# Added rows follow the scored rows by 24 places instead of 32 in the gather order of an expert layer

## The chip, the cores and the metric

The kernel runs on one core of one Trainium2 chip. The metric is device time in microseconds of one execution of the whole program. All data are fp32.

## The reference

The program computes a chain of transformer-like blocks on 256 tokens with 2048 channels (attention, a Fourier mixer, a convolution and state-space mixer, attention to a memory) and ends with an expert layer (PEER). Only this last layer is touched by the change:

```python
def peer(h, w_q, sub_keys, u_tab, v_tab):
    ...                                    # for each token and each of 8 heads: two top-16 lists, summed,
    top_s, pos = lax.top_k(cand_s, PEER_TOPK)   # and of the 256 sums the top 16
    idx = jnp.take_along_axis(cand_i, pos, axis=-1)
    g = jax.nn.softmax(top_s, axis=-1)
    ...
    def block(args):                       # 128 tokens, 8 x 16 = 128 experts for each
        xt, it, gt = args
        u = jnp.take(u_tab, it, axis=0)
        act = jax.nn.gelu(jnp.einsum("td,tkd->tk", xt, u))
        v = jnp.take(v_tab, it, axis=0)
        return jnp.einsum("tk,tkd->td", gt * act, v)
```

Then the layer's output is added to the residual stream and normalised with a gain. Each table has 16,384 rows of 2048 floats (8 KB).

## The kernel before, in words

The tokens lie in two tiles of 128, one token on each partition. For tile t and slot k (0 to 127, 16 for each head) one gather fetches, for each of the 128 tokens, its own row of a table: 128 rows of 8 KB, at most 1 MB. A gather of the first table (u) brings what is called here a **scored** row: VectorE multiplies it by the token's vector and sums it to one number per token (line 3779, one fused instruction). A gather of the second table (v) brings an **added** row: it is multiplied by its weight and added to the output. Slots with an exactly zero weight get an index beyond the table, and those tokens' rows are left out of the transfer.

- **Gathers** are issued by GpSimd (lines 3892 for u, 3896 for v), in the order that `gather_order` writes out and that all engines follow. There are 12 buffers. Gather n (after the start) takes the buffer of gather n - 12 and waits until that row is used. A scored row's gather waits besides for its head's indices (`idx`); an added row's gather waits for `rows_needed` of its head, the indices in which the zero weights are marked.
- **The order** begins with `LAG` scored rows. Then one added row and one scored row alternate until the scored rows are out; the last `LAG` added rows stand alone.
- **VectorE** (`v_experts`) walks through the same order. A scored row is multiplied and summed. Behind each head's 16th scored row comes `v_cubic` (four small instructions, lines 3739 to 3745), and `WEIGHTS_BEHIND = 4` places later `v_weights` (lines 3754 to 3763), the last of which writes `rows_needed`. The choice of the experts for the next pair of heads is laid beside the scored rows k = 0, 2, ... 18 of each 32 (`choice_at`), in ten steps. After the last added row of a tile `v_finish` adds the sums (line 3790), takes the norm and scales (line 3796).
- **ScalarE** (`a_experts`) computes the tanh for each head right behind that head's last scored row (line 3828), the exponentials of a choice (line 3690), and for each added row that TensorE takes a diagonal matrix with the weights (line 3837, four buffers). It works in order: diagonals behind a tanh wait for the tanh.
- **TensorE** adds the rows: `diag @ row` in four products of 512 columns, which accumulate in four PSUM banks (line 3579). While both kinds of rows alternate it takes the slots with k % 8 = 1 to 7 and VectorE those with k % 8 = 0 (line 3726). Of the rows of the second tile that stand alone (`added_alone`) TensorE takes k % 8 = 1, 3, 5, 7 and VectorE the even ones.

For the first two heads the experts are chosen head by head before the gathers begin; from the third head on a slot whose softmax weight is exactly zero is skipped in the u table as well.

Of the kernel before, what the change touches and what calls it, by code (L numbers as in the profile page):

```python
# [37 lines left out]
E_HEADS, E_KEYS, E_HALF, TOPK = 8, 128, 64, 16  # L38
# [3402 lines left out]
        return [key for q in (ch // 4, ch // 4 + 1) for key in turn_free(("ffn_x", q), 4, NT)]  # L3441


LAG = 2 * TOPK
PE_ROWS = (1, 2, 3, 4, 5, 6, 7)
PE_ROWS_ALONE = (1, 3, 5, 7)
WEIGHTS_BEHIND = 4
# [3 lines left out]
def gather_order():  # L3451

    scored = [(t, 0, k) for t in range(NT) for k in range(E_SLOTS)]
    added = [(t, 1, k) for t in range(NT) for k in range(E_SLOTS)]
    order = scored[:LAG]
    for n in range(len(added)):
        order.append(added[n])
        order += scored[LAG + n:LAG + n + 1]
    return order
# [10 lines left out]
def added_alone(t, k):  # L3470

    return (t, k) >= (NT - 1, E_SLOTS - LAG)

# [579 lines left out]
```

## Time and profile before

| | us |
|---|---|
| median of 3 runs | 3149.53 |
| lowest, highest | 3142.96, 3149.68 |
| the profiled execution, whole | 3139.42 |
| its span from first to last instruction | 3138.1 |
| first gather of the expert layer | 2093.34 |
| last gather issued | 3107.52 |

TensorE is busy for 90% of the span, VectorE for 72%, GpSimd for 37%, ScalarE for 33%. These are averages over stages with different limits. The expert layer is the last third of the span and is read by itself. Places in the code are given as the lines of the kernel (L3892 is line 3892); "releaser" is the instruction or transfer on which a wait ended.

### The profile page before, as it was taken

Reading aid. Unit: us, or ns where it says so; the run is one execution under the profiler, and the core shown is the slowest. Engines: PE = TensorE matmul, PEld = TensorE weight load, DVE = VectorE, ACT = ScalarE, POOL = GpSimd, SP = SyncE. Lnnn points to the kernel's source line nnn. Section 1 sums busy time; section 2 is a strip of 40 time slices with the busy share of each in tenths; the row PEclk is TensorE's granted clock in tenths of the full one; section 3 lists DMA queues with packets and bytes.
Section 4 is the critical chain, followed back from the end, with each engine's and each line's share of the span. In section 5 each row is a group of like instructions: output and inputs, shape, how many; then the busy total and the mean of one; then the engine's idle time right before and its main releaser. Section 6 shows DMA issues by size and latency. Waiting matters only on the chain.

```text
span 3138.1 us, 35531 instructions
## 1 busy us (share of the span) xinstructions
PE 2815.4 (90%) x12772; PEld 1974.2 (63%) x12772; DVE 2259.0 (72%) x3778; ACT 1047.5 (33%) x2133; POOL 1159.5 (37%) x1973
## 2 busy tenths in 40 slices
PE   6999999899999999999999999992888798888888
PEld 4667888556688888787876778882333333333333
DVE  5558888876667776556785565579978878888766
ACT  5454345234355545344523554421000010100001
POOL 6677877870000000000121000027555565554653
PEclk9999999999999999999999999996999899999999
DMA  9977585644647766555454474469999999999996
GB/s 377 387 282 267 213 278 188 242 168 161 199 130 257 244 219 200 182 189 208 155 176 134 165 239 133 174 232 418 417 418 417 418 414 414 402 418 411 417 416 248
DMA packets 297872, 865.10 MB, mean 276 GB/s; under 512 B 30249, under 2 KB 154537, under 8 KB 228009
## 3 DMA queue, kind: packets, MB, share of 16 engines
q1 hardware_dynamic: 216448, 417.56, 38.3%
q0 software_dynamic: 77024, 434.65, 34.1%
q10 hardware_dynamic: 4224, 10.62, 0.9%
q8 instruction: 101, 1.65, 0.2%
q14 instruction: 75, 0.61, 0.1%
HBM read 965.94 MB, written 17.96 MB: 314 GB/s over the span
## 4 chain that ended last, share of the span: by engine, by line
PE 61%; DVE 20%; DMA 12%; ACT 3%; issue 3%; POOL 1%; SPq 0%; ACTq 0%; POOLq 0%; DVEq 0%
PE lin L569 13%; PE lin L3579 8%; PE lin L571 6%; PE lin L494 6%; PE lin L496 6%; PE lin L495 6%; DVE arena L3779 5%; DMA arena<-in_peer_u,arena 4%; PE lin L395 4%; DMA ring<-in_peer_v,arena 3%; DMA ring<-in_peer_u,arena 2%; DVE scratch L916 2%; DMA arena<-in_peer_v,arena 2%; DVE weight_parts L452 2%; DVE ring L3779 1%
## 5 line engine op out<-in xcount | busy, mean ns | idle before, releaser
L452 DVE TENSOR_TENSOR weight_parts<-ring,weight_parts 128x512 fp32r<-128x512 f32 (+2 forms) x994 | 671.3, 689 | 468.2 <-ACT weight_parts L440 463.4
L440 ACT CAST weight_parts<-ring 128x512 fp32r<-128x512 f32 (+2 forms) x994 | 595.4, 609 | 696.9 <-PE lin L496 349.2
L569 PE MATMUL lin<-parts,weight_parts 128*128 128x512 f32 x1792 | 641.0, 401 | 12.7 <-DVE weight_parts L452 9.8
L3579 PE MATMUL lin<-ring,scratch 128*128 128x512 f32 x1136 | 529.8, 621 | 96.5 <-ACT scratch L3837 52.1
L571 PE MATMUL lin<-parts,weight_parts 128*128 128x256 f32 x1792 | 502.7, 281 | 0.0
L3579 PEld LDWEIGHTS lin<-ring,scratch 128*128 128x128 f32 x1136 | 220.6, 199 | 402.3 <-issue 343.3
L494 PE MATMUL lin<-weight_parts,parts 128*128 128x512 f32 (+2 forms) x1092 | 419.3, 384 | 22.3 <-DVE weight_parts L452 15.8
L3779 DVE CUSTOM_DVE_ANT_0 arena<-ring,aux 128x2048 f32<-128x2048 f32 x146 | 333.8, 2286 | 110.8 <-DMA ring<-in_peer_u,arena 106.9
L495 PE MATMUL lin<-weight_parts,parts 128*128 128x512 f32 (+2 forms) x1092 | 409.6, 375 | 0.0
L496 PE MATMUL lin<-weight_parts,parts 128*128 128x512 f32 (+2 forms) x1092 | 409.4, 375 | 0.0
L569 PEld LDWEIGHTS lin<-parts,weight_parts 128*128 128x128 f32 x1792 | 338.0, 189 | 109.8 <-DVE weight_parts L452 15.5
L3579 PE MATMUL lin<-arena,scratch 128*128 128x512 f32 x560 | 266.9, 627 | 106.4 <-ACT scratch L3837 82.7
L571 PEld LDWEIGHTS lin<-parts,weight_parts 128*128 128x128 f32 x1792 | 339.8, 190 | 0.4
L3892 POOL DMA_INDIRECT ring<-in_peer_u,arena x168 | 206.3, 1228 | 331.8 <-DVE arena L3596 230.8
L3579 PEld LDWEIGHTS lin<-arena,scratch 128*128 128x128 f32 x560 | 109.8, 201 | 258.6 <-issue 163.4
L494 PEld LDWEIGHTS lin<-weight_parts,parts 128*128 128x128 f32 x1092 | 207.4, 190 | 75.5 <-DVE weight_parts L452 25.0
L3837 ACT ACTIVATE scratch<-ident,arena 128x128 f32<-128x128 f32 x212 | 79.6, 398 | 507.7 <-PE lin L3579 475.3
L3896 POOL DMA_INDIRECT ring<-in_peer_v,arena x172 | 178.5, 1038 | 185.9 <-PE lin L3579 111.6
L496 PEld LDWEIGHTS lin<-weight_parts,parts 128*128 128x128 f32 x1092 | 207.4, 190 | 36.8
L495 PEld LDWEIGHTS lin<-weight_parts,parts 128*128 128x128 f32 x1092 | 207.8, 190 | 35.0 <-issue 1.1
L3779 DVE CUSTOM_DVE_ANT_0 arena<-arena,aux 128x2048 f32<-128x2048 f32 x74 | 169.2, 2286 | 50.5 <-DMA arena<-in_peer_u,arena 47.0
L1095 POOL DMA_DIRECT2D arena<-mem_turned x3 | 1.6, 543 | 538.9 <-PE aux L2324 528.7
(357 smaller groups left out, 3775.5 us busy)
## 6 DMA issues: line engine op xcount, KB each, us to landing
ring<-in_ada_row_loads SPq DMA_DIRECT2D x64, 1024.0 KB, 7.9
ring<-in_w_in_fourier SPq DMA_DIRECT2D x64, 1024.0 KB, 8.4
ring<-in_ada_front_loads SPq DMA_DIRECT2D x32, 1024.0 KB, 9.0
ring<-in_w_in_attn SPq DMA_DIRECT2D x32, 1024.0 KB, 6.0
ring<-in_w_out_fourier SPq DMA_DIRECT2D x16, 2048.0 KB, 8.1
ring<-in_w_in SPq DMA_DIRECT2D x24, 1024.0 KB, 7.5
ring<-in_mem_k_loads SPq DMA_DIRECT2D x16, 1024.0 KB, 10.9
ring<-in_w_out_attn SPq DMA_DIRECT2D x8, 2048.0 KB, 8.0
```

The costliest lines, as they stand in the source:

```text
L395: mm = c.nc.tensor.matmul(banks[j // 2][:, (j % 2) * SEQ:(j % 2 + 1) * SEQ], wt[:, k % L.kc, j * P:(j + 1) * P], rhs(k), start=(k == 0 and ...
L440: c.nc.scalar.copy(c.w_parts[:, q, 0, 0:L.per * w], weights_of(c, L, load, w, k)).then_inc(c.a_high.after(("high", L.name, i)), 1)
L452: c.nc.vector.tensor_tensor(c.w_parts[:, q, 1, 0:L.per * w], weights_of(c, L, load, w, k), c.w_parts[:, q, 0, 0:L.per * w].bitcast(F32), A ...
L494: c.nc.tensor.matmul(banks[t][:, 0:w], lhs(0, k, t), hi, start=(k % part == 0), stop=False)
L495: c.nc.tensor.matmul(banks[t][:, 0:w], lhs(0, k, t), lo, start=False, stop=False)
L496: mm = c.nc.tensor.matmul(banks[t][:, 0:w], lhs(1, k, t), hi, start=False, stop=(k % part == part - 1))
L569: c.nc.tensor.matmul(pairs(banks[j][:, :]), c.w_parts[:, q, 0, b], x, start=(k == 0), stop=False, skip_group_check=True)
L571: mm = c.nc.tensor.matmul(banks[j][:, hi_at * SEQ:(hi_at + 1) * SEQ], c.w_parts[:, q, 1, b], x[:, hi_at, :], start=False, stop=(k == L.K - ...
L3579: mm = nc.tensor.matmul(X.sums[t][b][:, :], c.diag[:, X.diag_of(t, k), :], X.buf_of[t, 1, k][:, b * 512:(b + 1) * 512], start=(k == PE_ROW ...
L3779: c.nc.vector.tensor_tensor_reduce(out=product, in0=buf, in1=hn, scale=1.0, scalar=0.0, op0=ALU.mult, op1=ALU.add, accum_out=X.act[:, t, k ...
L3892: c.nc.gpsimd.indirect_dma_start(X.bufs[q], None, X.tables[0], rows, bounds_check=E_KEYS * E_KEYS - 1, oob_is_err=False).then_inc(got[q].a ...
L3896: c.nc.gpsimd.indirect_dma_start(X.bufs[q], None, X.tables[1], rows, bounds_check=E_KEYS * E_KEYS - 1, oob_is_err=False).then_inc(got[q].a ...
```

## The change

`LAG` becomes 24 instead of 32. So the order begins with 24 scored rows, an added row follows the scored row of the same slot by 24 slots and not 32, and the last 24 added rows (k from 104 to 127 of the second tile) stand alone. The functions `gather_order` and `added_alone` read `LAG`; nothing else is edited.

```diff
-LAG = 2 * TOPK
+LAG = TOPK + TOPK // 2
 PE_ROWS = (1, 2, 3, 4, 5, 6, 7)
 PE_ROWS_ALONE = (1, 3, 5, 7)
 WEIGHTS_BEHIND = 4
```

## Rows read from the trace of the kernel before

**Rows 1.** Busy time by stage: us, PE, PEld, DVE, ACT, POOL, PEclk, DMA share, GB/s

```profile
2100.00:2125.00 25.00, 24.32 (x118) 21.04 (x117) 24.36 (x46) 2.13 (x5) 17.85 (x9) 1.00 1.01 422
...
2170.00:2690.00 520.00, 417.51 (x896) 174.35 (x896) 426.42 (x648) 47.77 (x133) 298.93 (x267) 0.91 1.01 417
2690.00:2715.00 25.00, 14.97 (x29) 6.59 (x30) 21.89 (x38) 6.42 (x15) 7.79 (x8) 0.73 0.96 368
2715.00:3065.00 350.00, 298.20 (x643) 124.31 (x642) 268.45 (x371) 30.17 (x84) 194.91 (x184) 0.94 1.01 416
3065.00:3115.00 50.00, 45.92 (x104) 19.98 (x103) 41.39 (x27) 7.72 (x19) 24.27 (x23) 0.97 0.88 325
3115.00:3138.10 23.10, 12.33 (x29) 5.13 (x27) 6.07 (x13) 3.10 (x9) 0.00 (x0) 0.88 0.11 46
```

**Rows 2.** DMA queue of the gathers: packets, MB, share of 16 engines

```profile
q0 software_dynamic: 77024, 434.65, 34.1%
```

**Rows 3.** Waits, 2100 to 3138.1 us: total us, times, longest

```profile
POOL ring L3896 <- PE lin L3579: 111.6, 72, 4.4
DVE arena L3779 <- DMA ring<-in_peer_u,arena: 106.9, 79, 2.9
...
DVE arena L3779 <- DMA arena<-in_peer_u,arena: 47.0, 36, 2.1
```

**Rows 4.** Timeline of the end: start us, us, engine, instruction

```profile
3047.31 0.99 POOL L3892 DMA_INDIRECT arena<-in_peer_u,arena  x1 [0.30 <-issue]
...
3063.18 0.99 POOL L3896 DMA_INDIRECT arena<-in_peer_v,arena  x1 [1.15 <-PE lin L3579]
...
3065.07 2.29 DVE L3779 CUSTOM_DVE_ANT_0 arena<-arena,aux 128x2048 f32<-128x2048 f32 x1 [1.78 <-DMA arena<-in_peer_u,arena]
...
3070.43 15.70 PE L3579 MATMUL lin<-ring,scratch 128*128 128x512 f32 x32 [4.08 <-ACT scratch L3837]
...
3073.79 0.17 DVE L3763 CAST arena<-arena 128x16 uint32<-128x16 f32 x1
...
3127.37 2.48 DVE L3790 TENSOR_TENSOR arena<-arena,lin 128x512 f32<-128x512 f32 x4 [12.58 <-PE lin L3579]
...
3070.43 56.91 PE lin L3579 x128
```

**Rows 5.** Timeline of GpSimd: the gathers 0, 23, 24, 27, 31 and 32

```profile
2093.34 1.07 POOL L3892 DMA_INDIRECT ring<-in_peer_u,arena  x1 [230.75 <-DVE arena L3596]
...
2144.01 0.99 POOL L3892 DMA_INDIRECT arena<-in_peer_u,arena  x1 [0.30 <-issue]
2145.31 2.14 POOL L3892 DMA_INDIRECT ring<-in_peer_u,arena  x1 [0.30 <-issue]
...
2154.05 0.99 POOL L3892 DMA_INDIRECT ring<-in_peer_u,arena  x1 [2.98 <-DVE arena L3779]
...
2166.76 2.28 POOL L3892 DMA_INDIRECT ring<-in_peer_u,arena  x1 [3.57 <-DVE arena L3779]
2169.34 1.91 POOL L3896 DMA_INDIRECT arena<-in_peer_v,arena  x1 [0.30 <-issue]
...
2193.68 3.01 POOL L3892 DMA_INDIRECT ring<-in_peer_u,arena  x1 [0.30 <-issue]
```

**Rows 6.** Timeline of VectorE: end of scored row 15, weights of head 0

```profile
2153.18 0.08 DVE L3779 DVE_READ_ACCUMULATOR2_ANT arena<- 128x1 f32 x1
...
2163.59 0.17 DVE L3763 CAST arena<-arena 128x16 uint32<-128x16 f32 x1
```

**Rows 7.** Busy time from the first gather's traffic on, columns of rows 1

```profile
2094.00:2159.10 65.10, 40.73 (x223) 35.31 (x221) 63.37 (x136) 8.72 (x23) 47.35 (x29) 0.85 0.99 403
```

**Rows 8.** The same in 2 us windows; the gain row's load

```profile
2094.00:2096.00 2.00, 2.00 (x11) 1.74 (x10) 1.86 (x10) 0.00 (x0) 1.42 (x2) 1.00 0.56 61
2096.00:2098.00 2.00, 2.00 (x11) 1.77 (x10) 1.89 (x7) 0.00 (x0) 1.67 (x2) 1.00 0.82 307
...
2131.46 0.35 SPq L3512 DMA_DIRECT2D arena<-in_final_norm_g  x1
```

**Rows 9.** GpSimd by line, 2166 to 2196 us, then 3047 to 3109

```profile
L3892 POOL DMA_INDIRECT ring<-in_peer_u,arena x5 | 11.0, 2201 | 4.8 <-DVE arena L3779 3.6 <-issue 1.2
L3896 POOL DMA_INDIRECT ring<-in_peer_v,arena x4 | 7.6, 1910 | 1.2 <-issue 1.2
...
L3896 POOL DMA_INDIRECT ring<-in_peer_v,arena x24 | 23.8, 991 | 20.2 <-PE lin L3579 9.2 <-issue 4.8 <-DVE aux L3726 3.9
```

**Rows 10.** Timeline: last step of a choice, VectorE after it, the finish

```profile
2640.53 0.32 ACT L3690 ACTIVATE arena<-arena,st 128x32 f32<-128x32 f32 x1 [9.66 <-DVE arena L3671]
...
2650.52 2.29 DVE L3779 CUSTOM_DVE_ANT_0 arena<-ring,aux 128x2048 f32<-128x2048 f32 x1 [1.24 <-DMA ring<-in_peer_u,arena]
...
2684.35 0.08 DVE L3779 DVE_READ_ACCUMULATOR2_ANT arena<- 128x1 f32 x1
...
2696.05 2.28 DVE L3779 CUSTOM_DVE_ANT_0 arena<-arena,aux 128x2048 f32<-128x2048 f32 x1
```

## The prediction

> **What bounds the kernel now.** I read the stages first, then the waits inside the expert stage, then its start and its end. In the windows by stage [rows 1] the reader is to look at the last two columns. From 2100 to 3065 us the 16 DMA engines are busy at a share of 0.96 to 1.02 and move 416 to 422 GB/s, whatever TensorE and VectorE do beside them; only after 3065 us does the rate fall to 325 and then 46 GB/s. So in this stage a time is lost when the gathers stop, and it is not won back later, because there is no idle DMA time to win it back in. The one large dip is 2690 to 2715 us with 368 GB/s. The totals say the same: the gathers' queue moved 434.65 MB [rows 2], and at 417 GB/s that is 1042 us, nearly the whole stage.
>
> The waits [rows 3] show who follows. VectorE waits for scored rows to land (106.9 + 47.0 us), GpSimd waits for a buffer that TensorE or VectorE frees, TensorE waits for the scaled diagonals of ScalarE. All of these are engines at the speed of the transfers.
>
> The end is another matter. The last scored row's gather is issued at 3047.31 and the row has landed when VectorE takes it at 3065.07; TensorE's last stretch begins at 3070.43 and runs without a gap for 56.91 us in 128 records [rows 4]. An added row on TensorE is 8 records (4 products, 2 passes each), so that is 16 rows: exactly the rows 97, 99, ... 127 of the second tile which the rule for rows that stand alone gives to TensorE. The first four took 15.70 us, the rest (56.91 - 15.70) / 12 = 3.43 us each. VectorE then waits 12.58 us for them [rows 4]. The end of the kernel is therefore: last scored row landed + 5.36 us + 16 TensorE rows + the finish.
>
> **The order in numbers.** Call the place in the gather order n, 0 to 511. Before, added row j stands at 32 + 2j and scored row 32 + j behind it; after the change they stand at 24 + 2j and 25 + 2j. Twelve buffers go round, so gather n waits until row n - 12 has been used. A head's weights are computed on VectorE four places behind its last scored row, and the added rows' gathers of that head wait for them, with everything behind them in GpSimd's queue.
>
> For head h of 1 to 15 (both tiles counted through) the last scored row stood at 32h - 1, now at 32h + 7; the weights were at 32h + 3, now at 32h + 11; the head's first added row was at 32h + 32, now at 32h + 24. The distance shrinks from 29 places to 13. Thirteen is still enough: the gather one place ahead, 32h + 23, waits for the scored row at 32h + 11, which VectorE takes after it has computed those weights. I cost these waits at nothing for heads 1 to 14. Two heads differ.
>
> **Head 0 (a new stall).** Its weights stay at place 19, since its rows 0 to 15 and the four behind them are all scored rows in both orders, but its first added row comes at 24, not 32. Gathers 24 to 31 were free to go from 2145.31 to 2166.76 [rows 5]. Now GpSimd stands at gather 24 until VectorE has written the indices at 2163.76 (2163.59 + 0.17) [rows 6]. The gathers 0 to 23 are all that the DMA engines have: 24 x 1.0486 MB (128 rows of 2048 floats; the first two heads skip none) and the 1.0486 MB of the final norm's gain row that SyncE loads at 2131.46 [rows 8], 26.2 MB. From 2094, where the queues had run dry, 403 GB/s x 65.1 us = 26.2 MB are moved at 2159.1 [rows 7]. So the engines run dry about 4.7 us before the weights are there. From a release to the issue it takes 0.87 us (row 15 used at 2153.18, gather 27 at 2154.05) [rows 5, 6]. From the very first issue at 2093.34 to the time at which full-rate traffic would have begun: between 2094 and 2098 (61 + 307) x 2 = 0.74 MB moved, 1.75 us at 420, so 2096.25, that is 2.9 us [rows 5, 8]. Dry time: 2163.76 + 0.87 + 2.9 - 2159.1 = 8.4 us. That is the lower bound. To it comes that GpSimd's descriptor work takes 1.91 to 2.20 us and not 0.99 while VectorE runs scored rows back to back [rows 9], as it will on the rows 19 to 23 that it has in hand: +0.9 for the first gather. And the issues then follow at 1.91 + 0.30 = 2.21 us, 4.42 a pair, where the transfers of a pair take 3.96 (below): 0.46 us lost a pair until VectorE has caught up. It is behind by five rows, so some two to four pairs: +1.2, at most +2; with a slow first issue (3.0 us are seen once in [rows 5]) 14 us is the upper end. I take 8.4 + 0.9 + 1.2 = **10.5 us**. Before, the same slow issues did no harm, because some five gathers lay queued.
>
> The Trainium skill ("DMA: Bandwidth & Descriptors", Specifications) gives about 1 us to the first byte for DMAs issued by GpSimd; by that the restart would cost 1.9 us less and the sum would be 8.6. The rows of this trace have 2.9 from issue to traffic, and the measurement decides; the 1.9 us lie inside the forecast's own range below and change no chance. The Trainium skill ("SBUF — State Buffer", SBUF: two separate sides) says that VectorE and GpSimd hold a shared port pair exclusively and that descriptors are then late; the 1.91 against 0.99 us agrees, and by it the refill stays slow as long as VectorE has rows in hand.
>
> **The last head.** Its weights come at place 491, and gather 496 (row 112) waits for them; the buffer alone would let it go at row 484. Going by today's gather in the same place behind the last scored row (3063.18, nine behind it) it could go 2 us before that row is taken; it is now held until 8.9 us after (3065.07 to the end of the weights at 3073.96) [rows 4]. In front of it 8 added rows are queued, 8 x 1.4 = 11 us of transfers, and TensorE is busy with the rows 105 to 111 until 5.4 + 15.7 = 21 us; row 113 lands by 15. Nothing is lost; without that cover it would be 2 to 3 us.
>
> **The end (a gain and what it costs).** Alone are 24 rows, 12 of them on TensorE: 4 x 3.43 = 13.7 us less. But eight more added rows are transferred ahead of the last scored one, and in a saturated stage that delays it by their transfer time. An added row moves less than 1 MB, since slots whose weight is zero are skipped. How much: from row 32's place to the last scored row, 3065.07 - 2179 (2159.1 + 8 x 2.5 us) gives 886 us for 448 rows, 1.98 each, 3.96 a pair; less 2.5 for a full scored row leaves 1.46. In the tail 325 GB/s x 50 us = 16.3 MB for 32 rows [rows 1], 0.51 MB or 1.21 us at 418 GB/s, while by the DMA share it is 50 x 0.88 / 32 = 1.38. I take 1.42 x 8 = 11.4 us; bounds 1.21 and 1.98, 9.7 and 15.8 us. Net end: 11.4 - 13.7 = **-2.3 us** (-4.0 to +2.1). Rows 96 to 103 now go 7 to TensorE and 1 to VectorE in the shared stretch: 7 x 3.43 in 8 x 3.96 us, hidden behind the transfers.
>
> **The middle.** The finish of the first tile moves from place 286 to 278, which is 9 places and not 25 behind the last step of a choice. In the same cycle VectorE waits for transfers again at 2650.52, 10 us after that step at 2640.53 [rows 10]; nine places are 18 us, so it should have caught up. The stall at 2690 to 2715 costs (417 - 368) x 25 / 417 = 2.9 us today [rows 1], since the next choice begins at once; after the change eight quiet pairs follow. I put it at 0, from -3 to +4.
>
> **Sum.** 10.5 - 2.3 + 0 = +8.2 us, with bounds 8.4 - 4.0 - 3 = +1.4 and 14 + 2.1 + 4 = +20. The profiled execution took 3139.42 us (span 3138.1 and 1.3 around it) and would be 3147.6. It lies 10.1 us under the median of the runs, 3149.53, which so becomes **3157.7**.
>
> **Rivals.**
> - *The shorter end decides, faster.* If the scored rows ran at the speed of TensorE or VectorE, eight rows moved ahead of the last one would be hidden and the whole 13.7 us be won. Against it stands the DMA share of 1.01. It gives 10.5 - 13.7 = -3.2, 3146.3; it decides once the first stall is under 13.7 us, and beats 0.2% if the stall is under 7.4 us, for which the queue would have to hold out two microseconds past 2159. Chance 0.09.
> - *No stall at head 0* because the queue is deeper than its bytes say: -2.3 us, 3147.2. Against it the byte count, which closes on 26.2 MB. Chance 0.07.
> - *The finish collides with the choice.* VectorE is still three or more rows behind at place 278, and its stall of 11.7 us (2684.35 to 2696.05) [rows 10] empties the queue as well: 5 to 8 us more, 3163 to 3166. Chance 0.15.
> - *The wait bites at every head*, not once: only if GpSimd passed 32h + 23 without VectorE, which the buffer rule excludes. Each would cost a part of 8 us, 15 of them up to 100. Chance 0.02.
>
> **How the numbers follow.** The forecast has 0.67. Its own range is 3152 to 3164. The range of all, 3149 to 3167, takes in the collision and a part of the cheap cases. A measurement of this kernel tells about 0.2% (6.3 us) from no change. The forecast lies beyond that in some 6 of 10 of its cases, the collision always, the two cheap cases fall within it or rarely below: slower 0.57, within 0.36, faster 0.07.
>
> **What would show it.** In the profile after: a gap in GpSimd's gathers of about 19 us before the first gather of the second table, at some 2164 us; a DMA share well under 1 near 2159 to 2168, TensorE's first added rows near 2175 instead of 2194; the last stretch of TensorE 96 records and 43 us long; from the last scored row to the end 13.7 us less, and that row itself some 22 us later. The prediction is wrong if the DMA share stays at 1 across 2160 us, if that gap recurs at each head, or if the last scored row lands less than 15 or more than 30 us later.

## The result, and the profile after

The change makes the kernel slower: median 3166.56 us (3158.14 to 3170.93, 5 runs) against 3149.53 us (3142.59 to 3150.98, 5 runs), ratio 1.0057 with a 95% interval of 1.0044 to 1.0070, that is +18.0 us (13.9 to 22.0). The forecast was 3157.7 us with a range of 3149 to 3167, that is +8.2 us. The direction was right and the time is just inside the range, but the size was less than half of the measured one. The profiled execution of after took 3158.14 us, its span is 3156.8 us, 18.7 more than that of before; 2.25 of them lie ahead of the first gather (2095.59 against 2093.34), in code that is the same, so 16.4 us belong to the change. In the traces below the first gather starts anywhere from 2093 to 2113 us; so all traces are laid on each other at that gather.

The start. Timeline of GpSimd in the kernel after, to be read beside [rows 5] with 2.25 us to be taken off: gathers 23, 24 and 25, then two later ones.

```profile
2146.25 0.99 POOL L3892 DMA_INDIRECT arena<-in_peer_u,arena  x1 [0.30 <-issue]
2166.74 2.26 POOL L3896 DMA_INDIRECT ring<-in_peer_v,arena  x1 [19.50 <-DVE arena L3763]
2169.31 1.91 POOL L3892 DMA_INDIRECT ring<-in_peer_u,arena  x1 [0.30 <-issue]
...
2182.64 2.49 POOL L3892 DMA_INDIRECT ring<-in_peer_u,arena  x1 [0.30 <-issue]
2185.44 0.99 POOL L3896 DMA_INDIRECT arena<-in_peer_v,arena  x1 [0.30 <-issue]
```

The reader should look at the second line: GpSimd sat idle for 19.50 us before the first gather of the second table, released by line 3763, the last instruction of head 0's weights. The busy time by stretch shows what that does to the transfers (last two columns: DMA share and GB/s; over the same stretches the kernel before has 418 to 422 GB/s):

```profile
2160.00:2170.00 10.00, 0.00 (x0) 0.00 (x0) 9.30 (x19) 1.60 (x5) 2.96 (x2) 0.50 0.22 76
2170.00:2195.00 25.00, 13.94 (x26) 5.59 (x27) 18.38 (x17) 1.21 (x3) 21.34 (x13) 0.76 0.92 338
2195.00:2215.00 20.00, 14.10 (x32) 5.62 (x31) 13.01 (x14) 1.39 (x5) 17.26 (x10) 0.95 1.02 416
```

The first line is the dry queue, the stretch in which the DMA engines have no gather left: 10 us at 76 GB/s lose 10 x (1 - 76/420) = 8.2 us. The second is the refill, in which gathers are issued again but the transfers are not yet back at their rate. The prediction took it too lightly: 25 us at 338 GB/s lose another 4.9 us.

The middle. Timeline of VectorE at the finish of the first tile, after. Before, the wait was 2.81 us and VectorE went on with scored rows at 2696.05 [rows 10].

```profile
2688.35 2.48 DVE L3790 TENSOR_TENSOR arena<-arena,lin 128x512 f32<-128x512 f32 x4 [6.96 <-PE lin L3579]
...
2697.14 2.28 DVE L3779 CUSTOM_DVE_ANT_0 arena<-ring,aux 128x2048 f32<-128x2048 f32 x1
```

VectorE stands 6.96 us waiting for TensorE's last rows of the tile. Why TensorE is late shows in its own timeline, the first two lines from the kernel after, the third from the kernel before:

```profile
2660.31 8.70 PE L3579 MATMUL lin<-ring,scratch 128*128 128x512 f32 x16 [7.86 <-ACT scratch L3837]
2670.87 3.70 PE L3579 MATMUL lin<-ring,scratch 128*128 128x512 f32 x8 [1.87 <-ACT scratch L3837]
...
2659.74 3.67 PE L3579 MATMUL lin<-arena,scratch 128*128 128x512 f32 x8 [1.10 <-DMA arena<-in_peer_v,arena]
```

After the change TensorE waits for ScalarE's diagonals until 2660.31 and again until 2670.87, and from there it works without a gap up to the finish at 2688.35. Before, the same two waits ended at 2630.63 and 2641.20, and from 2659.74 on TensorE waited for transfers again, which means that it had caught up well before the finish at 2687.24.

The end. The chain that ended last, after, to be read beside [rows 4]: the transfer of the last scored row, VectorE's last scored rows, the last stretch of TensorE.

```profile
3077.34 19.20 DMA ring<-in_peer_u,arena
...
3096.56 2.31 DVE arena L3779 x2
...
3101.87 44.13 PE lin L3579 x96
```

96 records are 12 rows in place of 16, and 44.13 us in place of 56.91. The last head's gather is held as well (timeline of GpSimd, after):

```profile
3106.20 0.99 POOL L3896 DMA_INDIRECT ring<-in_peer_v,arena  x1 [14.00 <-DVE arena L3763]
```

From 3100 to 3110 us the transfers fall to 137 GB/s behind this wait, so the queue runs low here as well; but TensorE has rows in hand and runs through.

**An account by events.** VectorE's 256 scored rows are the same in all kernels. For each I take the time at which the row ends (the start of its accumulator read) in one kernel minus that in the kernel before, with the first gathers laid on each other. A column is one execution, and it scatters by up to some 2 us where two orders are the same (e2 stands at 14.2 at row 225 and at 16.5 at row 236). Where eight more added rows have been transferred ahead of a scored row, their time is in the difference. Rows 48 to 150 and from 172 on are the quiet stretches; between lies the first tile's finish. The last line is the end: from the last scored row's end to the first instruction of the finish, against 60.1 us before.

```
scored row        after  e1    e2    e3    e4    e5    e6    e7    e8
 19               -0.1   0.0  -0.1   0.0  -0.3   0.2  -1.0   0.0  -0.4
 31               16.3   0.0  15.5   0.0   9.0  12.6  18.8   2.2  14.5
128               26.1  -0.4  14.6  11.4  19.7  20.3  27.8  13.3  25.7
172               28.8   0.2  14.3  14.7  22.1  24.1  30.8  17.1  25.3
255               29.2  11.8  16.5  15.4  22.7  25.1  31.6  18.7  26.0
end, us           47.2
```

For after it says: 26.1 us by row 128 (the start and eight added rows), 3.1 us more from there on, and 60.1 - 47.2 = 12.9 us won at the end: 26.1 + 3.1 - 12.9 = 16.3, which is, but for the rounding, the 16.4 us of the spans. Row 255 is not a lucky place to read: over rows 172 to 255 the difference lies between 26.8 and 31.1, with a mean of 28.9.

### The profile page after: what moved, and what is told of

Same layout as the page of the kernel before. It is cut to its first block, busy times and chain, and to the rows that moved or that the text cites. A ratio compares the mean times of both kernels' runs of the same rounds, so it can differ in the third digit from the quotient of the medians.

```text
span 3156.8 us, 35586 instructions
## 1 busy us (share of the span) xinstructions
PE 2833.0 (90%) x12796; PEld 1979.7 (63%) x12796; DVE 2253.9 (71%) x3775; ACT 1043.9 (33%) x2136; POOL 1151.8 (36%) x1973
## 4 chain that ended last, share of the span: by engine, by line
PE 60%; DVE 18%; DMA 13%; issue 4%; ACT 3%; POOL 2%; SPq 0%; another core or an unknown queue 0%; ACTq 0%; POOLq 0%; DVEq 0%
PE lin L569 13%; PE lin L3579 7%; PE lin L494 7%; PE lin L496 6%; PE lin L495 6%; PE lin L571 6%; DMA ring<-in_peer_u,arena 6%; DVE arena L3779 5%; DMA ring<-in_peer_v,arena 4%; PE lin L395 4%; DVE scratch L916 2%; DVE weight_parts L452 1%; DMA arena<-in_peer_u,arena 1%; PE lin L2689 1%; PE aux L695 1%
## 5 line engine op out<-in xcount | busy, mean ns | idle before, releaser
L3579 PE MATMUL lin<-ring,scratch 128*128 128x512 f32 x1152 | 542.8, 624 | 150.0 <-DMA ring<-in_peer_v,arena 101.4
```

The source lines that it names most:

```text
L3579: mm = nc.tensor.matmul(X.sums[t][b][:, :], c.diag[:, X.diag_of(t, k), :], X.buf_of[t, 1, k][:, b * 512:(b + 1) * 512], start=(k == PE_ROW ...
```

## The experiments

Line numbers in the experiments are up to nine higher than in before, since lines were put in above. Every experiment was run beside fresh runs of the kernel before; its ratio is to these, and its difference in us is the ratio less 1, times 3148.

### e1: the shorter distance only at the end

The edit is on the kernel after.

```diff
+def lag_at(n):
+    return max(24, min(32, 32 - (n - 152) // 4))
 def gather_order():
...
-    order = scored[:LAG]
+    order, done = [], 0
     for n in range(len(added)):
+        ahead = min(len(scored), lag_at(n) + n)
+        order += scored[done:ahead]
+        done = max(done, ahead)
         order.append(added[n])
-        order += scored[LAG + n:LAG + n + 1]
     return order
```

> The order of before (32 places) up to added row 152, past the finish of the first tile; from there the distance shrinks by one in every four added rows to 24, and the last 24 added rows stand alone. My theory (head 0 stalls the gathers at the start, the finish of tile 0 waits longer for TensorE, the end gains a little): neither of the two losses is here, so only the end is left, eight added rows of transfer (11.4 us) against four TensorE rows less (13 us): -4 to 0 us against the kernel before. Rival (the loss sits in the end itself, because the last head's gather waits for its weights): +5 us or more. The gathers show no gap at 2145 to 2165 us.

Measured: 1.0001 (0.9989 to 1.0014), +0.3 us. As expected. The eight added rows are in the table: nothing until row 172, 11.8 us at row 255. TensorE's last stretch (chain of e1):

```profile
3091.18 43.18 PE lin L3586 x96
```

So the end is eight added rows of 12 us against 56.91 - 43.18 = 13.7 us, a draw, and the wait of the last head's gather costs nothing there.

### e2: the shorter distance only at the start

```diff
-LAG = TOPK + TOPK // 2
+LAG = 2 * TOPK
...
+def lag_at(n):
+    return max(24, min(32, 24 + (n - 32) // 4))
```

(shown against after, with the same loop as e1; so against before only the function and the loop are new)

> The order of after (24 places) up to added row 32, then the distance grows by one in every four added rows back to 32, with 32 added rows alone at the end. My theory: the whole stall at head 0 is here and nothing else, +13 us against the kernel before (+11 to +16). Rival (idle transfer time is won back later, or the stall costs only the 8.4 us of the dry queue): under +9 us.

Measured: 1.0042 (1.0030 to 1.0054), +13.2 us. The table has 14.6 us at row 128, 14.3 at row 172 and 16.5 at row 255: once the queue has run dry, nothing is won back in 900 us. This is the price of the start alone. The windows of e2 repeat those of after:

```profile
2174.00:2184.00 10.00, 0.00 (x0) 0.00 (x0) 9.30 (x19) 1.60 (x5) 2.93 (x2) 0.50 0.23 83
2184.00:2209.00 25.00, 13.96 (x28) 5.64 (x29) 18.41 (x17) 1.21 (x3) 21.40 (x12) 0.78 0.94 346
```

### e3: 32 scored rows ahead, then the shorter distance

```diff
+def lag_at(n):
+    return max(24, min(32, 32 - n // 4))
```

(on after: `LAG` stays 24, so 24 rows stand alone; the same loop)

> As after, but 32 scored rows stand ahead of the first added row; the distance shrinks to 24 over the first 32 added rows. My theory: no stall at the start, the finish of tile 0 stands where it stands in after: +1 to +6 us against the kernel before, some 13 us less than after. If the start is not the cause, it is as slow as after (+17).

Measured: 0.9998 (0.9985 to 1.0011), -0.6 us with an interval of -4.7 to +3.5; the expectation began at +1, so the estimate missed it by little, and the interval reaches into its lower half. The start is what makes the change slow: without the stall the rest is a draw. By its trace the eight rows cost 11.4 us (row 128), the middle 4.0 (row 255 less row 128).

### e4 and e6: the weights of head 0 earlier and later

```diff
 def weights_at(n):
...
+    if n < TOPK + 8:
+        return (0, 0) if n == TOPK - 1 + 2 else None
     done = ORDER[n - WEIGHTS_BEHIND] if n >= WEIGHTS_BEHIND else None
```

(e4, on after; in e6 `+ 6` stands in place of `+ 2`)

> After, with the weights of head 0 of the first tile computed 2 and not 4 places behind its last scored row, so that the gather of added row 0 may go some 7 us earlier (about 2157 instead of 2165 us into the time of before). My theory: the dry time falls from about 8 to about 1 us and part of the slow refill stays: 6 to 10 us less than after, +7 to +11 against before. Rival (the position of the first added row and not its wait costs the time, for example by the slow descriptor work): as slow as after.

> After, with the weights of head 0 of the first tile computed 6 and not 4 places behind its last scored row: two scored rows of VectorE later, 2 x 2.21 us. My theory (the wait for these weights is the cause): 3 to 5 us slower than after. Rival (the place of the first added row costs the time): no change against after.

Measured: e4 1.0044 (1.0025 to 1.0063), +13.9 us; e6 1.0060 (1.0039 to 1.0080), +18.9 us. In the traces e4's row 128 lies 6.4 us earlier than after's, and row 255 6.5 us. The runs say 4 us less than after, with intervals that overlap, so of the size expected (6 to 10) only the lower edge is met, and that by the trace alone. e6 is 1.7 to 2.4 us later than after in the table, less than the 3 to 5 expected; its runs can't be told from after's. GpSimd's waits are what the edits were meant to change: 13.32 us in e4 (the line below), 19.50 in after, 23.93 in e6.

```profile
2170.21 2.27 POOL L3898 DMA_INDIRECT ring<-in_peer_v,arena  x1 [13.32 <-DVE arena L3765]
```

What each wait costs is read best from the transfers, over the same 55 us behind the first gather in each kernel: first after, then e4, e5 (below) and e6.

```profile
2160.00:2215.00 55.00, 28.04 (x57) 11.22 (x58) 40.69 (x49) 4.19 (x13) 41.55 (x23) 0.78 0.83 319
2169.95:2224.95 55.00, 34.97 (x69) 14.29 (x70) 45.34 (x53) 4.48 (x14) 46.51 (x28) 0.80 0.93 357
2166.57:2221.57 55.00, 30.80 (x61) 12.72 (x62) 44.77 (x56) 4.18 (x13) 33.38 (x30) 0.75 0.86 345
2162.75:2217.75 55.00, 28.36 (x56) 11.14 (x56) 38.38 (x48) 3.19 (x10) 37.15 (x23) 0.74 0.75 292
```

The kernel before moves 419 GB/s in this stretch and e2 319, as after does. Against 419, after loses 55 x (1 - 319/419) = 13.1 us, e4 8.1, e5 9.7 and e6 16.7. So the time lost follows the wait for the weights, in both directions, but not one for one: the wait is 6.2 us shorter in e4 and 5.0 us are saved, 4.4 us longer in e6 and 3.5 more are lost. In e6 VectorE has three rows in hand and not five when the gathers start again, and so may disturb the refill less; that is argued, not shown by a run of its own.

### e5 and e9: the refill

```diff
 def scores_from_psum(t, k):
-    return k >= (2 * TOPK if t == 0 else 4)
+    return k >= (TOPK if t == 0 else 4)
```

(e5 on after, e9 on before. The same function also sends these rows' products to another place in SBUF, so the edit changes that as well.)

> After, with one edit: the scored rows of the first tile read the token's vector from PSUM from row 16 on (before and after: from row 32 on). So VectorE has one SBUF operand less in the rows 19 to 31, during which the gathers are started again. My theory (after the dry time GpSimd's own work for a gather, 1.9 to 3.0 us while VectorE reads two SBUF operands, keeps the transfers under full rate until scored row 32): GpSimd's time for a gather falls to about 1.0 us from the first added row on, and the start costs 4 to 6 us less than in after, some 9 instead of 14 us. Rival (the refill is slow by itself, small transfers and their latency with an empty queue): no change against after.

> The kernel before (32 places) with the edit of the PSUM experiment alone: scored rows of the first tile read the token's vector from PSUM from row 16 on. My theory (slow descriptor work costs nothing as long as gathers lie queued): no change, within 2 us, and the transfers stay at full rate from 2145 to 2200 us. If that edit is a gain by itself: 4 us or more faster, and then it says nothing on the refill.

Measured: e5 1.0033 (1.0022 to 1.0045), +10.4 us, 7.6 less than after; e9 0.9994 (0.9982 to 1.0007), no change. GpSimd by line, first e5 from 2173 to 2223 us, then after from 2166.5 to 2216.5, 50 us each (busy us, mean ns of one):

```profile
L3892 POOL DMA_INDIRECT ring<-in_peer_u,arena x11 | 12.9, 1172 | 3.9 <-issue 2.1 <-DVE arena L3779 1.5 <-PE lin L3579 0.3
L3896 POOL DMA_INDIRECT ring<-in_peer_v,arena x11 | 10.9, 989 | 25.9 <-DVE arena L3763 19.8 <-PE lin L3579 3.7 <-issue 2.4
```

```profile
L3892 POOL DMA_INDIRECT ring<-in_peer_u,arena x8 | 18.0, 2249 | 2.4 <-issue 2.4
L3896 POOL DMA_INDIRECT ring<-in_peer_v,arena x8 | 11.9, 1494 | 21.6 <-DVE arena L3763 19.5 <-issue 2.1
```

In the same stretch a gather takes on average 1172 and 989 ns in place of 2249 and 1494. The dry stretch stays and the refill is quick (windows of e5, 71 and then 395 GB/s in place of 76 and 338):

```profile
2166.50:2176.50 10.00, 0.00 (x0) 0.00 (x0) 9.02 (x19) 1.60 (x5) 2.31 (x3) 0.50 0.22 71
2176.50:2201.50 25.00, 16.37 (x34) 6.88 (x35) 21.36 (x18) 1.20 (x3) 19.23 (x19) 0.76 0.98 395
```

The table has 5.8 us less than after at row 128 and 4.1 at row 255, and the transfers of the 55 us say 3.4; so e5 takes away more than half of the loss behind the dry stretch, and on how much more the measures don't agree. And e9 says that the edit is nothing by itself. Its window shows GpSimd busy for 8.88 of 25 us, where it is busy for 21.65 in before (2167 to 2192 us), and the transfers at the rate that they have in before anyway:

```profile
2175.00:2200.00 25.00, 0.00 (x0) 0.00 (x0) 23.08 (x34) 0.32 (x1) 8.88 (x9) 0.50 1.02 422
```

With gathers queued the slow descriptor work is covered.

### e7: 28 places

```diff
-LAG = TOPK + TOPK // 2
+LAG = 28
```

> The distance is 28 places. My theory: four more scored rows are queued when GpSimd stops at the first added row, so the transfers do not run dry, and a slow refill of 1 to 3 us is left; the end is 4 x 1.47 = 5.9 us of transfer against two TensorE rows (6.9 us); the finish of the first tile waits for TensorE between 2.8 and 7 us: 0 to +4 us against the kernel before. If the loss grew in proportion to the places taken off, it would be +8 to +9.

Measured: 1.0022 (1.0010 to 1.0035), +6.9 us (3.1 to 11.0), more than the 0 to +4 expected. The queue does not run dry, as expected, but the refill costs nearly as much as in after (4.9 us) although nothing was dry (windows of e7):

```profile
2170.00:2180.00 10.00, 0.00 (x0) 0.00 (x0) 9.30 (x19) 1.31 (x4) 2.97 (x2) 0.50 1.01 422
2180.00:2215.00 35.00, 18.84 (x35) 7.81 (x36) 33.31 (x39) 1.79 (x6) 29.52 (x19) 0.73 0.98 375
```

35 x (1 - 375/420) = 3.8 us. GpSimd waited 9.46 us for the weights; the queue must have shrunk to almost nothing by then, and with 2.21 us from one gather to the next it was not filled again while VectorE read rows from SBUF. The middle and the rest of the 6.9 us I can't split by this run.

### e8: the finish of the first tile later

```diff
     for n, (t, table, k) in enumerate(ORDER):
+        if n >= 6 and ORDER[n - 6] == (0, 1, E_SLOTS - 1):
+            yield from v_finish(c, X, 0)
...
-        if k == E_SLOTS - 1:
+        if k == E_SLOTS - 1 and t == NT - 1:
             yield from v_finish(c, X, t)
```

> After, with the finish of the first tile moved six places later in VectorE's order, behind three more scored rows and one added row. My theory (the middle costs 3 us because VectorE stands 6.96 us waiting for TensorE's last rows of the tile, where it stood 2.81 before): the wait at the finish is gone or under 2 us, 3 to 6 us less than after. Rival (the time goes in the finish's own work and the stop of the gathers behind it): 0 to 1 us less than after, or more time, since TensorE gets its banks back later.

Measured: 1.0048 (1.0033 to 1.0063), +15.1 us, 2.9 less than after, just under the 3 to 6 expected; the intervals overlap, so the runs alone don't prove it. The traces bear it out: no wait is left at the finish,

```profile
2698.47 2.48 DVE L3792 TENSOR_TENSOR arena<-arena,lin 128x512 f32<-128x512 f32 x4
```

and from row 128 to row 255 the table grows by 0.3 us in place of 3.1. Means are firmer than single rows: from rows 120 to 149 to rows 172 to 255 the mean difference grows by 2.2 to 2.9 us in after, e3, e4, e5 and e6, and by none in e8 (-0.7) and in e12 (-0.3), which has the later finish too.

### e10, e11, e12: the end with TensorE relieved

The end is bound by TensorE's rows in all these kernels. e10 (on before) gives VectorE five of eight rows that stand alone, e11 adds the later finish (three places), e12 is e3 with the same three of eight rows on TensorE and the finish six places later:

```diff
-PE_ROWS_ALONE = (1, 3, 5, 7)
+PE_ROWS_ALONE = (1, 4, 7)
```

> The kernel before (32 places) with TensorE taking three of eight rows that stand alone (k % 8 = 1, 4, 7) and VectorE five: 12 TensorE rows x 3.43 us + 2 and 20 VectorE rows of some 2.45 us behind the last scored row. My theory (the end is bound by TensorE's 16 rows): VectorE's chain of 3 + 1 + 20 x 2.45 = 53 us takes over from 62.3: 7 to 10 us faster. Rival (the transfers of the last rows, landed some 47 us after the last scored row, or GpSimd's issue bound it): under 4 us.

> The same with the finish of the first tile three places later in VectorE's order (behind one scored and one added row), so that the 2.81 us of waiting for TensorE are filled: 1 to 3 us less than the kernel with three of eight alone, 9 to 12 us less than the kernel before.

> 32 scored rows at the start, distance 24 from added row 32 on, the finish of the first tile six places later, TensorE taking three of eight of the 24 rows alone (9 rows). My theory: last scored row 11.8 us (eight added rows) and 1 us (finish) later, then VectorE's 15 rows, 3 + 1 + 15 x 2.45 = 41 us in place of 62.3: 6 to 10 us faster than before. Rival (the last head's gathers, held for the weights, now bound the end since TensorE no longer covers them): 4 us or more slower than that.

Measured: e10 3139.29 us, 0.9977 (0.9965 to 0.9989), -7.2 us (-11.0 to -3.5); e11 3137.49 us, 0.9971 (0.9961 to 0.9981), -9.1 us; e12 3144.40 us, 0.9989 (0.9978 to 1.0001), -3.5 us. e10 and e11 are as expected and are faster than both kernels; the 1.9 us between them are within their intervals. e12 missed its -6 to -10, and the rival had it. With TensorE no longer the cover, the last head's held gathers bind the end (timeline of GpSimd and of VectorE's last add, e12):

```profile
3096.27 0.99 POOL L3905 DMA_INDIRECT ring<-in_peer_v,arena  x1 [13.27 <-DVE arena L3772]
...
3115.72 0.99 POOL L3905 DMA_INDIRECT ring<-in_peer_v,arena  x1 [0.30 <-issue]
...
3130.88 2.48 DVE L3799 TENSOR_TENSOR arena<-arena,lin 128x512 f32<-128x512 f32 x4 [2.12 <-PE lin L3586]
```

The wait starves the transfers a second time, 114 GB/s for 10 us (window of e12):

```profile
3088.00:3098.00 10.00, 6.07 (x10) 2.60 (x11) 9.51 (x15) 3.38 (x8) 1.43 (x2) 0.83 0.30 114
```

The 16 gathers behind it go out one every 1.3 us, the last one is issued at 3115.72, and TensorE, which now waits for rows to land, takes the last at 3127.17.

## Why the forecast was right in sign and wrong in size

| term | forecast | measured | from |
|---|---|---|---|
| start: dry queue | 8.4 | 8.2 | windows of after |
| start: first issue and refill | 2.1 | 4.9 to 6.5 | windows of after; row 128 less e3's 11.4 and the dry part |
| eight added rows | 11.4 | 11.4 to 12 | e3, e1 |
| the middle | 0 | 3.1 | row 255 less row 128; e8 |
| the end of TensorE | -13.7 | -12.9 | last scored row to finish |
| sum | 8.2 | 16.3 | |

The measured sum closes by the table of events: start 26.1 - 11.4 = 14.7, eight added rows 11.4, the middle 3.1, the end -12.9. So of the 8.1 us by which the forecast was short, 4.2 lie in the start, 3.1 in the middle and 0.8 in the end.

**The stall at head 0** was right in place, releaser and length: GpSimd idle for 19.5 us where some 19 were forecast, transfers dry where the byte count put it, and none again before 2169.5, 2.8 us behind the first issue. e2 and e3 show that it alone makes the change slow, e4 and e6 that it follows the place of the weights.

**The refill is the term that failed first**, by its size: 2.1 us with the first issue, at least 4.9 measured. The step read: 0.46 us are lost a pair "until VectorE has caught up", "some two to four pairs: +1.2". VectorE did catch up then (its first wait for a row is at 2181.98). But the slow issues did not end with it: as long as VectorE's scored rows read both operands from SBUF, that is up to row 31, a gather issued beside one takes about 2 to 3 us. I had the kernel's own rule for this (scored rows read PSUM from row 32 on) and did not use it as the end of the slow stretch. From 2182 to 2195 us, at 358 GB/s, 1.9 us are lost this way. The 12 us before, at 315 GB/s, lose 3.0, so the price of the stretch that I did count was too low as well. 4.42 us a pair against 3.96 was too kind: the first seven distances are (2182.64 - 2166.74) / 7 = 2.27 us, 4.54 a pair. That a small added row is done before the next gather has been issued may be the rest; no run splits it off. e5 takes most of the cause away, e9 shows that it costs nothing where gathers are queued.

The Trainium skill ("SBUF — State Buffer", SBUF: two separate sides) has this as a rule: a GpSimd-issued DMA starves when VectorE holds the shared port pair. e5 agrees, 2249 against 1172 ns on average in the same stretch. The Trainium skill's figure of about 1 us to the first byte ("DMA: Bandwidth & Descriptors", Specifications) would have made the start cheaper; the dry part measured, 8.2 us, is that of the 2.9 us from the trace.

**The middle failed second.** The step read: VectorE waits for transfers again 10 us after the choice's last step, "so it should have caught up", cost 0. VectorE had, if only just: in e8, where it goes on with scored rows at this place, the next one (row 151) waits 0.70 us for its transfer. TensorE had not: the finish waits for TensorE, whose backlog from the choice was still there nine places later, so the wait grew from 2.81 to 6.96 us. I looked at the engine that does the finish and not at the one for which it waits. e8 takes the wait away and the 3 us with it.

**The end** was right but for 0.8 us: 12 TensorE rows, the last scored row later by eight rows of transfer, and no loss from the last head's held gather, as e1 confirms. TensorE's stretch was 44.13 and not 43.2 us.

**Waits at the heads 1 to 14** cost nothing that can be seen: in after the difference lies between 23.0 and 26.7 us from row 48 to row 128 and between 26.8 and 31.1 from row 172 to row 255. A drift of a microsecond or two is in the scatter, but no head adds a stall that lasts.

The rivals: that no stall comes fell with the profile after, that the end decides with e1, e2 and e3. That the finish collides was half right, with another mechanism and 3 us in place of 5 to 8.

Two sums of the prediction don't hold. Its bounds add up to +20 us, which is 3169.5, and yet its range ends at 3167; that the time lies inside by 0.4 us is luck and no merit of the mechanism. And for the stall to be under 7.4 us in place of 10.5 the queue would have to hold out three microseconds more, not two.

What stays open: why e6's rows are only some 2 us later than after's when its transfers lose 3.5 us more, how much of the refill is left without the slow issues, and how e7's 6.9 us divide.

## What to carry to other kernels

When a stage is bound by transfers, each place where the issuing engine stops must be held against what is queued, in bytes; and a queue that has run empty, or nearly, costs a second time, because slow issues that were hidden behind it now set the rate until they end. When a wait is moved, look at the backlog of the engine that it waits for, not only at the one that waits. An order by a constant distance has its worst spot where it begins: the same distance behind a longer head (e3) lost nothing.

## What the runs showed of the hardware

A GpSimd gather of 128 rows of 8 KB takes 0.99 us of GpSimd's time, and 1.9 to 3.0 us beside a VectorE instruction of 128x2048 that reads two tensors from SBUF; with one of the two in PSUM it takes 0.99 again (e5, e9). In the tail of the kernel before, three windows of 10 us from 3080 to 3110 have a DMA share of 0.94, 0.97 and 0.96 with only 323, 363 and 353 GB/s, while the mixed stretch has 417 at 1.01: gathers in which many rows are skipped seem to keep the DMA engines busy beyond their bytes. No run tests this. I had used 1.42 us an added row, between the figure by bytes and that by share, and the measured 11.4 to 12 us for eight bear the higher one out: 1.42 to 1.5 us a row.
